# A hybrid decoder layer on eight cores: small transposes moved from TensorE to DMA, with block-wide gate sums and three column groups by rows at the end

## The reference

```python
proj = x @ w_in          # q,k (512 each), v,g (1024 each), gate rank 16, q_s 1024, k_s 128, v_s 128
gk = log_sigmoid(gk_lo @ w_gk2 + b_gk) / 16           # per key channel, <= 0
# gated linear attention, 4 heads, dk 128, dv 256, over chunks; b = cumsum(gk) within a chunk
o     = (q*exp(b)) @ state + tril((q*exp(b)) @ (k*exp(-b)).T) @ v
state = state*exp(b_last) + (k*exp(b_last - b)).T @ v
gla   = o * rsqrt(mean(o*o) + eps) * norm_w * silu(g)
# sliding window of 128 with a learned sink, 16 query heads on 2 key/value heads of 64,
# over banded blocks: softmax over the previous and the current block of 128 keys
swa   = softmax_with_sink(q_s @ k_s.T / 8) @ v_s
x = layer_norm(ALPHA*x + concat(gla, swa) @ w_out)
x = layer_norm(ALPHA*x + square(relu(x @ w_up)) @ w_down)     # d_ff = 8192
```

## Time and profile before

| | before |
|---|---|
| median of 3 runs | 2823.77 us |
| profiled execution, its own time | 2822.92 us |
| its span, first to last instruction of the slowest core | 2821.4 us |
| cores | 2810.8 to 2821.4 us |
| PE busy | 2726.7 us (97%) |
| DVE, ACT, POOL busy | 1013.9, 630.1, 125.1 us |

### The profile page before, as it was taken

The page is one execution under the profiler, slowest core; times in us unless marked ns, Lnnn a source line. Parts: engine busy times, 40 slices in busy tenths (PEclk is TensorE's granted clock), DMA queues, the critical chain, the costliest instruction groups (busy, mean ns, idle before and its releaser), DMA issues.

```text
span 2821.4 us, 37826 instructions; the slowest of 8 cores (2810.8 to 2821.4 us)
## 1 busy us (share of the span) xinstructions
PE 2726.7 (97%) x14367; PEld 1363.0 (48%) x14608; DVE 1013.9 (36%) x1480; ACT 630.1 (22%) x1347; POOL 125.1 (4%) x227
## 2 busy tenths in 40 slices
PE   6999999999999999999999999999999999999987
PEld 3446674444444444444444676444444444444433
DVE  2553545751211212121257444582211211221138
ACT  3434655331001001001003555332101101100100
POOL 2000000000000000000000000000000000000000
PEclk9999999999999999999999999999999999999998
DMA  9674445635454354445578334734354344335342
GB/s 153 84 122 75 78 89 99 144 78 92 69 88 75 60 90 75 75 69 89 83 121 194 75 63 104 159 81 90 60 90 77 73 74 91 75 60 90 75 75 120
DMA packets 50913, 256.24 MB, mean 91 GB/s; under 512 B 4656, under 2 KB 21552, under 8 KB 22192
## 3 DMA queue, kind: packets, MB, share of 16 engines
q0 software_dynamic: 44400, 211.47, 45.1%
q1 hardware_dynamic: 6336, 42.35, 4.2%
HBM read 448.47 MB, written 16.78 MB: 165 GB/s over the span
## 4 chain that ended last, share of the span: by engine, by line
PE 90%; DVE 4%; issue 2%; ACT 2%; DMA 2%; POOL 0%; DVEq 0%; ACTq 0%; POOLq 0%; SPq 0%
PE ps L292 88%; PE ps L295 1%; DVE racc L323 1%; ACT racc L312 1%; DVE racc L449 1%; DMA rexu<-w_kv 1%; DMA y<-racc 1%; DVE racc L315 0%; DMA wring<-w_down 0%; ACT rext L312 0%; ACT racc L327 0%; DVE rext L315 0%; DVE bnst L967 0%; ACT small L312 0%; DVE rexu L315 0%
## 5 line engine op out<-in xcount | busy, mean ns | idle before, releaser
L292 PE MATMUL ps<-wring,xreg 128*128 128x512 bf16 (+1 forms) x6594 | 1234.8, 346 | 12.2 <-DMA wring<-w_down 7.1
L292 PE MATMUL ps<-xreg,wring 128*128 128x512 bf16 (+1 forms) x5443 | 1200.8, 380 | 14.6 <-ACT racc L312 5.2
L292 PEld LDWEIGHTS ps<-wring,xreg 128*128 128x128 bf16 x6688 | 651.3, 98 | 583.0 <-issue 23.9
L292 PEld LDWEIGHTS ps<-xreg,wring 128*128 128x128 bf16 (+1 forms) x5568 | 539.5, 98 | 654.1 <-issue 21.0
L312 ACT ACTIVATE tmpr<-ps 128x512 f32<-128x512 f32 (+1 forms) x320 | 177.9, 556 | 1407.2 <-PE ps L292 1404.6
L315 DVE TENSOR_TENSOR xreg<-tmpr 128x512 bf16<-128x512 f32 x256 | 177.1, 692 | 705.0 <-ACT tmpr L312 705.0
L315 DVE TENSOR_TENSOR racc<-racc,ps 128x512 f32<-128x512 f32 x240 | 164.8, 687 | 507.9 <-PE ps L292 455.9
L323 DVE SCALAR_TENSOR_TENSOR racc<-racc,ps 128x512 f32<-128x512 f32 x128 | 87.8, 686 | 221.9 <-PE ps L292 221.6
L323 DVE SCALAR_TENSOR_TENSOR racc<-racc,small,rext 128x2048 f32<-128x2048 f32 x64 | 149.5, 2338 | 4.4 <-DVE racc L323 2.0
L292 PE MATMUL ps<-xreg 128*128 128x512 bf16 (+1 forms) x532 | 114.5, 373 | 0.6
L312 ACT ACTIVATE small<-small 128x1 f32<-128x1 f32 x192 | 38.7, 202 | 321.2 <-DVE small L826 312.4
(11 more groups left out here) (94 smaller groups left out, 934.0 us busy)
## 6 DMA issues: line engine op xcount, KB each, us to landing
wring<-w_up POOLq DMA_DIRECT2D x64, 1024.0 KB, 10.1
wring<-w_down POOLq DMA_DIRECT2D x64, 1024.0 KB, 10.0
wring<-w_gla POOLq DMA_DIRECT2D x26, 1024.0 KB, 9.4
racc<-x_own SPq DMA_DIRECT2D x16, 1024.0 KB, 12.6
y<-racc SPq DMA_DIRECT2D x16, 1024.0 KB, 4.2
xreg<-xT_prev POOLq DMA_DIRECT2D x16, 512.0 KB, 32.1
xreg<-xT_own POOLq DMA_DIRECT2D x16, 512.0 KB, 16.2
wring<-w_qs POOLq DMA_DIRECT2D x8, 1024.0 KB, 10.8
```

What stands on the lines that cost most here:

```text
L292: P.add("pe", lambda h: h.matmul(out, lhsT=lhsT, rhs=rhs, start=start, stop=stop), [lhsT, rhs], [out])
```

## The change

It has these parts.

1. `dtr` is new: an SP DMA with transpose, SBUF to SBUF, on one of 12 semaphores in turn. It makes `vs` from `vsT_h`, `kd_tok` from `kdT` and the columns of `mixT` from `gla_h`. The PE transposes for them and the copies out of PSUM are gone, and so are the two generator steps at the end of `gla_chunks`. In the last group of queries the double step of `g3` stands at i = 4 alone.
2. In `prev_state` the gates are summed over a block of 512 tokens with a pattern of ones; `negcC` has one column per block, and one exponential over 512 columns takes the place of four over 128. The pattern with resets (`scanpat`) is loaded when `prev_state` ends. Block 0's rows are all copied by DVE. The window's projections of block 0 stand behind block 1's keys, with `wkv_prev` in a part of xreg that the last block's x takes afterwards. The loads are reordered accordingly.
3. In the last part of the second pass only q = 0 goes by column groups, and q = 1, 2, 3 go tile by tile; the weights of q = 1, 2 are loaded into the free half of xreg. `ln2_last` splits the last tile's norm and store into two halves of columns.
4. `issue_x(3)` stands for `issue_x(2)` in the down-projection.

```diff
--- before.py
+++ after.py
-        wkv_prev = EX[:, 0:4096].rearrange("p (k n) -> p k n", n=256)
+        wkv_prev = XV[0][:, :, 512:768]
...
+            tctr = [0]
+
+            def dtr(out, in_):
+                i = tctr[0] % 12
+                tctr[0] += 1
+                P.add("sp", lambda h: h.dma_start(out=out, in_=in_, transpose=True), [in_], [out], stream=f"t{i}")
...
-            dma("sp", "c3", pat_f[:], scanpat, [], [pat_f[:]])
+            memset(pat_f[:], 1.0)
...
             def prev_state():
                 wks = [load_w(w_gla[h * 3][:, 0:2048], 16, 128) for h in range(4)]
+                queue_half(xT_prev, 1, 0, 1, 0)
+                issue_x(4)
                 load_piece("c8", wkv_prev, w_kv[:, 0:4096])
-                queue_half(xT_prev, 1, 0, 1, 0)
                 queue_half(xT_prev, 0, 1, 0, 0)
-                queue_half(xT_prev, 0, 0, 0, 1)
-                issue_x(12)
-                dma("pool", "c6", masks_b[:].rearrange("p a b -> p (a b)"), masks, [], [masks_b[:]])
-                wcap[0] = 6
+                issue_x(4)
                 blocks = [XV[1][:, :, 512:1024], XV[1][:, :, 0:512], XV[0][:, :, 0:512], XV[0][:, :, 512:1024]]
...
-                        cp("act" if tq % 2 else "dve", x_tok[:, tq, kg2 * 1024:(kg2 + 1) * 1024], bkb)
+                        cp("act" if tq % 2 and b else "dve", x_tok[:, tq, kg2 * 1024:(kg2 + 1) * 1024], bkb)
...
-                    ts(negcC[:, :, s0:s0 + 4], c_f.rearrange("p h (c t) -> p h c t", t=128)[:, :, s0:s0 + 4, 127],
-                       -1.0 / 16.0, None, ALU.mult, ALU.bypass)
-                    for j in range(s0 + 3, s0 - 1, -1):
-                        if b > 0 or j < 7:
-                            tt(negcC[:, :, j], negcC[:, :, j], negcC[:, :, (j + 1) % 8], ALU.add)
+                    ts(negcC[:, :, b], c_f[:, :, s0 * 128 + 511], -1.0 / 16.0, None, ALU.mult, ALU.bypass)
+                    if b:
+                        tt(negcC[:, :, b], negcC[:, :, b], negcC[:, :, b - 1], ALU.add)
...
-                        for j in range(4):
-                            act(tf[:, j * 128:(j + 1) * 128], c_f[:, h, (s0 + j) * 128:(s0 + j + 1) * 128], AF.Exp,
-                                bias=negcC[:, h, s0 + j:s0 + j + 1], scale=1.0 / 16.0)
+                        act(tf, c_f[:, h, s0 * 128:s0 * 128 + 512], AF.Exp, bias=negcC[:, h, b:b + 1], scale=1.0 / 16.0)
...
                 rows = keys(0)
-                bk = next_bank()
-                for kc in range(16):
-                    mm(bk[:, 0:128], wkv_prev[:, kc, 0:128], blocks[0][:, kc, 384:512], kc == 0, kc == 15)
-                ks_copies(bk, 0, 128)
                 rows(3)
-                bk = next_bank()
-                for kc in range(16):
-                    mm(bk[:, 0:128], blocks[0][:, kc, 384:512], wkv_prev[:, kc, 128:256], kc == 0, kc == 15)
-                cp("act", vs[:, 0, :], bk[:, 0:128])
                 for b in range(4):
...
                     if b == 0:
+                        bk = next_bank()
+                        for kc in range(16):
+                            mm(bk[:, 0:128], wkv_prev[:, kc, 0:128], blocks[0][:, kc, 384:512], kc == 0, kc == 15)
+                        ks_copies(bk, 0, 128)
+                        bk = next_bank()
+                        for kc in range(16):
+                            mm(bk[:, 0:128], blocks[0][:, kc, 384:512], wkv_prev[:, kc, 128:256], kc == 0, kc == 15)
+                        cp("act", vs[:, 0, :], bk[:, 0:128])
+                        queue_half(xT_prev, 0, 0, 0, 1)
+                        issue_x(4)
+                        dma("pool", "c6", masks_b[:].rearrange("p a b -> p (a b)"), masks, [], [masks_b[:]])
                         for h in range(2):
                             load_piece(f"wo{h}", wv_prev[h], w_gla[h * 3 + 1])
+                        wcap[0] = 6
+                        if wplan is not None:
+                            issue_w()
...
+                dma("sp", "c3", pat_f[:], scanpat, [], [pat_f[:]])
...
                         cp("act", vsT_h[half], bv[:, :])
+                        dtr(vs[:, 1 + half * 4:5 + half * 4, :], vsT_h[half])
                         yield
                         bk = next_bank()
                         proj_fm(w1, 0, 128, half, bk)
                         ks_copies(bk, 128 + half * 512, 512)
                         yield
-                        bkb = next_bank()[:, :].bitcast(BF16)
-                        for j in range(4):
-                            tr(bkb[:, j * 128:(j + 1) * 128], vsT_h[half][:, j * 128:(j + 1) * 128])
-                        cp("act", vs[:, 1 + half * 4: 5 + half * 4, :], bkb[:, 0:512].rearrange("p (t e) -> p t e", t=4))
...
-                    def kd_transposes(half):
-                        bkb = next_bank()[:, :].bitcast(BF16)
-                        for j in range(4):
-                            tr(bkb[:, j * 128:(j + 1) * 128], kdT[half][:, j * 128:(j + 1) * 128])
-                        cp("act", kd_tok[hb][:, half * 4:(half + 1) * 4, :], bkb[:, 0:512].rearrange("p (t d) -> p t d", t=4))
...
                         tt(kdT[half], bk[:, :], tf, ALU.mult)
+                        dtr(kd_tok[hb][:, half * 4:(half + 1) * 4, :], kdT[half])
...
                         stt(gla_h[t % 4], bo[:, 0:256], rs, gw[:, t, :], ALU.mult, ALU.mult)
-
-                    def tpose(t):
-                        bkb = next_bank()[:, :].bitcast(BF16)
-                        for ec in range(2):
-                            tr(bkb[:, ec * 128:(ec + 1) * 128], gla_h[t % 4][:, ec * 128:(ec + 1) * 128])
-                        cp("act" if t % 2 else "dve", mixT[:, 2 * h:2 * h + 2, t * 128:(t + 1) * 128],
-                           bkb[:, 0:256].rearrange("p (e t) -> p e t", e=2))
...
-                    for t in range(10):
-                        if t > 1:
-                            tpose(t - 2)
-                        if t < 8:
-                            chunk(t)
+                    for t in range(8):
+                        chunk(t)
                         yield
...
-                    if i in (2, 4, 6):
+                    if i == 4:
...
+                def ln2_last(t):
+                    mu, rs = stats(t)
+                    rows = slice(tok0 + t * 128, tok0 + (t + 1) * 128)
+                    cuts = [slice(0, D)] if t < 7 else [slice(0, 1024), slice(1024, D)]
+                    for c in cuts:
+                        stt(acc[t][:, c], acc[t][:, c], mu, gbc[:, c], ALU.subtract, ALU.mult)
+                    for i, c in enumerate(cuts):
+                        stt(acc[t][:, c], acc[t][:, c], rs, bbc[:, c], ALU.mult, ALU.add)
+                        dma("sp", f"z{t}" if i else f"y{t}", y[rows, c], acc[t][:, c], [acc[t][:, c]], [])
...
                     rows = s == 3 and pi == 1
-                    for q in range(2 if rows else 4):
+                    early = [[], []]
+                    if rows:
+                        for i in range(4):
+                            wv = XR[(p + 1) % 2][:, i * 4096:(i + 1) * 4096].rearrange("p (k n) -> p k n", n=512)
+                            load_piece(f"wo{i}", wv, w_down[s * 8 + 2 + i])
+                            early[i // 2].append((None, wv))
+                    for q in range(1 if rows else 4):
                         wd = down_w(q)
-                        issue_x(2)
+                        issue_x(3)
...
-                        wds = [down_w(q) for q in (2, 3)]
+                        wds = early + [down_w(3)]
                         for t in range(8):
-                            for i in range(2):
-                                down_unit(2 + i, t, wds[i])
-                            drive(ln2(t))
-                        for wd in wds:
-                            release_w(wd[0][0])
-                            release_w(wd[1][0])
+                            for i in range(3):
+                                down_unit(1 + i, t, wds[i])
+                            ln2_last(t)
+                        for wi, _ in wds[2]:
+                            release_w(wi)
```

More of the change, by code:

```diff
@@ L258, in build_program @@
         x1b = [EY[:, i * 2048:(i + 1) * 2048] for i in range(2)]
+        XV = [XR[i][:, :].rearrange("p (k t) -> p k t", k=16) for i in range(2)]
         x_tok = RA[:, 12288:20480].rearrange("p (t e) -> p t e", e=2048)
@@ L268, in build_program @@
         bbc = f32v(EX, 4096, 2048)
-        XV = [XR[i][:, :].rearrange("p (k t) -> p k t", k=16) for i in range(2)]
         acc = [f32v(RA, t * 4096, 2048) for t in range(8)]
@@ L1000, in record @@
                 do_pass(p)
-            P.add("sp", lambda h: h.nop(), [T("stream", f"y{t}") for t in range(8)], [])
+            P.add("sp", lambda h: h.nop(), [T("stream", f"{c}{t}") for c in "yz" for t in range(8)], [])
             return wlog
```

6 lines of the change are left out of this document (2 added, 4 removed).

## The result

Four runs of the changed kernel gave 2789.49 to 2793.67 us, median **2792.07 us**; the kernel before, 2822.16 and 2823.77 us. The ratio is 0.989, 95% interval 0.987 to 0.991: 1.1% or 31 us faster, less than the 2% that count as a change. (Some executions of every kernel here are disturbed and take some 60 us or more longer; no comparison uses them.) The profiled execution took 2789.49 us, 33.4 less than the one before, with a span of 2787.9 us. Its slowest core is 5, before it was 0.

The account below looks back on a forecast made before the run. TensorE, busy 97% of the span, was taken to bound the kernel. Gains of 11.4 + 7.6 + 7.2 + 14.4 - 2.0 = 38.6 us, subtracted from 2822.9, gave 2784 us, range 2766 to 2818.

Parts of the forecast that it names:

- A: Both passes: 208 fewer TensorE transposes at 55 ns each, 11.4 us gained.
- C: Waits inside the passes, at head 1's second key transposes and the last query group: 7.2 us gained, 3 to 11.
- E: New waits on transposes behind residual loads and at the second pass's gates: -2 us, -6 to 0.
- one double chunk less is sure (2 x 1.0): Last query group: three double chunks become one, so one 1.0 us state wait surely goes in each pass.
- signs of being wrong: Listed refutations: late weights in heads, DVE waiting for transposes, last query group keeping 6 us of waits, clock falling elsewhere.
- B: State before the first own block: shorter gate chain, fewer waits, full clock in block 0; 7.6 us gained, 4 to 9.
- D: End of second pass: early weights, DVE keeping up, shorter tail, split last store; 14.4 us gained, 13 to 20.4.
- the term for the fifth weight piece: End of second pass: last early w_down piece lands late, costing 3 us wait and 3 us of half clock.
- Rival 1: Transposes fill the DMA engines in the heads, delaying weights: up to 2922 us; 0.09 beyond 2880, 0.17 shared for 2800 to 2880.
- Rival 2: Transposes at times take over 15.7 us, so DVE blocks on gla_h: 2791 to 2808 us; shares 0.17 for 2800 to 2880.

Follow-up runs that it names:

- masks early: Changed kernel with the masked scores of heads 1 to 3 made one step earlier; 0.990 of the kernel before, 2788.0 to 2794.4 us and one of 2816.2.
- swapped banks: Changed kernel with each chunk taking the PSUM bank of its state update before that of its output; 2790.7 to 2794.1 us.
- changed kernel again: The changed kernel unaltered, run as control on the same chip as two other runs; 2792.3 to 2793.9 us, 0.9875 of the kernel before.
- end-only kernel: Kernel before with only the changes at the end of the second pass (early weights, groups by rows, split last norm); ratio 0.9936, 18 us gained.
- state only: Kernel before with only the `prev_state` changes (gate sums over 512, loads reordered); ratio 0.9972, 8 us gained.
- values by TensorE: Changed kernel with the 16 transposes of the banded values done by TensorE again; 0.9882 of the kernel before.
- values late: Changed kernel with the values' two transposing DMAs issued behind each pass's gates; 0.9862 of the kernel before, 2787.8 to 2791.2 us.
- both combined: Changed kernel with update's bank first, masked scores a step early, and values either on TensorE (0.9856 of before) or by DMA behind the gates (0.9827).
- transposes only: Kernel before with only the 208 small transposes moved from TensorE to DMA; ratio 0.9983, 5 us gained.
- own grain: Changed kernel with banded values tracked in 256-byte pieces, so the second value transposition doesn't wait for the first; 0.9906 of before, 2796 to 2799 us.
- combined, values late: Changed kernel with update's bank first, masked scores a step early, values' DMAs behind the gates; 0.9827 of the kernel before, 2778.8 to 2781.8 us.

## Why the prediction was right or wrong

The time came 8 us above the forecast and in its range, and the sum (38.6 against 33.4 us) looks better than its terms: one was 6 us too small and others together 11 us too large. That they cancel is luck.

- **A, C and E** were to give 11.4 + 7.2 - 2.0 = 16.6 us over both passes; they gave 5.6 us in the profile and 5 us alone. A's price of 55 ns is right where TensorE is the bound: heads 2 and 3 of the first pass, with 24 transposes fewer each, came out 1.24 and 1.33 us shorter (24 x 0.055 = 1.32). The step that failed is C's, that a wait goes when the instruction that stood in it goes. At the first chunk the transposes stood in front of a later wait of the same chain: ScalarE's exponentials, VectorE's keys, then the mask. They left, and PE waited 1.58 us for the mask in place of 0.91 + 0.21: from the start of the product before it to the chunk it was 5.12 us (286.19 to 291.31) and is 5.19 (277.87 to 283.06). The run with the masks early shows it. In the last group "one double chunk less is sure (2 x 1.0)" was wrong as a gain: the state's waits did fall by 1.8 us, but the bank of the chunk's output is taken next by the query projection, with or without the transposes' bank (by the count of banks a step, ten before and nine now, the transposes' ahead of it), and the waits there rose by 3.5. The swapped banks show that. C's 5.0 us in the groups came to nothing: the groups got 1.7 us shorter in the mean of eight cores, which A's 32 transposes alone account for (1.8), and on the profiled pair not even that, since the clock fell in the second pass as well. Two of the prediction's own signs of being wrong came true: the group kept its 6 us of waits, and the clock fell at a new place.
- **B**, 7.6 us: 7.5 us in the profile, 8.3 with the part alone. Its steps hold: the block 0 wait at 1.26 us, full clock behind it.
- **D**, 14.4 us with a top of 20.4: 20.7 us. DVE keeping up was right. Mis-sized was the term for the fifth weight piece, 3 us of wait and 3 at half clock, taken from a burst in a fuller queue (7.3 us a piece); here five pieces took 31 us from first issue, 6.3 each, and the last landed 0.5 us before its use. That the profiled core paid nothing is luck: on the other cores of this execution the wait is 0 to 3.0 us, in the changed kernel again 0.6 to 3.4, in the end-only kernel 0.9. Behind most of these waits PE ran on at full clock, but not behind all. Core 4 of the changed kernel again, where half a product (1.89 us at full clock) took 2.91:

```profile
2702.12 2.91 PE L292 MATMUL ps<-xreg 128*128 128x512 bf16 x8 [3.43 <-DMA xreg<-w_down]
```

- **E**, -2 us: the gates alone cost 1.5 us in the profiled pair and 1.4 to 2.4 us by the mean of the cores. The cause was not the queue order that I gave but the slower landing of the store, and for 0.65 us the earlier arrival of ScalarE. The residual loads ahead of the outputs cost nothing: DVE waited for no buffer.
- **Rival 1** needed 1.08 us of the engines a block; it was 0.18 to 0.25. The 1309 ns of the Trainium skill ("VectorE: DVE Perf Modes", "The three transpose paths") is no time of the engines here; as latency, 2.5 us for two blocks, it is not contradicted. "Advanced Engine Details and Errata" of the Trainium skill says under "X-Bar Transpose (TRN2)" that transposing DMAs are as fast as others. Here they were not: by bytes a block was to be 0.12 us, and it took 0.18 to 0.25. That is far from what rival 1 needed all the same.
- **Rival 2** (latency) fell: 2.5 us, where 15.7 were allowed. In the full queue of the second pass it was 14.4 us and more, for the values, where nobody waits.

## What to carry to other kernels

Before a wait is booked as gained, find its second-latest releaser: here the mask behind the keys, and the bank behind the state. Waits of 1 us in a row can cost more than their sum, since a unit at half clock behind them (5.31 or 5.86 us for 3.62) is worth two of them; with waits taken out of the row such units became rare. Compare a stretch over all cores, not between the two slowest: the same edit gave 6.9 us by the one and 3.9 by the other. Small transpositions by DMA are nearly free for the engine that bounds the kernel, if none is in flight beside a transfer that someone waits for.

## What the hardware showed that I had not expected

A 128x512 transposition by DMA beside weight loads (the 16 DMA engines 96% busy from 1475 to 1500 us in the changed kernel) lengthens the landing of a neighbouring 1 MB store. The mean landing over eight cores was 13.6 to 14.8 us with none in flight (before, end only, state only, values by TensorE, values late, both combined), 15.5 to 18.3 with one (changed, again, transposes only, banks swapped), 22.7 with two (own grain). Single cores overlap: 13.3 to 16.6 us before, 12.6 to 18.5 in the changed kernel. By bytes a transposition is an eighth of the store. What in the DMA engines causes it was not tried.

The granted clock in the last group doesn't follow from the waits alone. Number of the eight cores whose product at this place (behind the first waits of the group) lasted 4.6 us or more in place of 3.6, and how long the group takes where none did:

| kernel | first pass | second pass | group without a slow unit, us |
|---|---|---|---|
| before | 8 | 0 | 45.0 to 45.2 |
| end only | 8 | 6 | 45.2 |
| state only | 4 | 7 | 44.8 to 45.0 |
| transposes only | 8 | 4 | 44.1 to 44.3 |
| changed | 6 | 5 | 43.8 to 44.1 |
| changed, again | 7 | 5 | 43.9 to 44.1 |
| values late | 7 | 8 | 44.1 |
| banks swapped | 1 | 4 | 42.5 to 42.8 |
| masks early | 2 | 2 | 43.4 |
| combined, values late | 0 | 1 | 42.1 |

The end and the state alone leave this group's instructions as they are, and the counts still change. So part of the loss in the second pass isn't of the edit of the group. What decides it on a core was not found. In the second pass the end-only kernel had a unit of 6.24 us, and the kernel before, behind the same waits of 1.00 and 1.50 us, one of 3.63. Its timeline:

```profile
1760.47 0.59 PE L292 MATMUL ps<-racc,ksT 64*128 64x512 bf16 x2 [1.50 <-DVE rexu L323]
1760.99 3.63 PE L292 MATMUL ps<-xreg,wring 128*128 128x512 bf16 x16
```
